# Feed-forwards with one 512-column matmul over both parts of the input, in a fused kernel of three transformer blocks

## The reference

```python
def _swiglu(x, w_gate, w_up, w_down):
    return (jax.nn.silu(x @ w_gate) * (x @ w_up)) @ w_down

x = x + 0.5 * _swiglu(_rmsnorm(x, ffn1_norm[l]), ffn1_w_gate[l], ffn1_w_up[l], ffn1_w_down[l])
```

## Time and profile before

| | us |
|---|---|
| median of 3 runs (lowest to highest) | 4005.26 (3999.87 to 4008.55) |
| span of the profiled execution | 4004.4 |
| PE busy | 3909.7 (98%) |
| PE loading weights | 3793.3 (95%) |
| DVE busy | 2736.3 (68%) |
| ACT busy | 1987.8 (50%) |

### The profile page before, as it was taken

The page is one execution under the profiler, slowest core; times in us unless marked ns, Lnnn a source line. Parts: engine busy times, 40 slices in busy tenths (PEclk is TensorE's granted clock), DMA queues, the critical chain, the costliest instruction groups (busy, mean ns, idle before and its releaser), DMA issues.

```text
span 4004.4 us, 78708 instructions
## 1 busy us (share of the span) xinstructions
PE 3909.7 (98%) x34150; PEld 3793.3 (95%) x34150; DVE 2736.3 (68%) x4071; ACT 1987.8 (50%) x2620; POOL 212.2 (5%) x277
## 2 busy tenths in 40 slices
PE   8999999999999999999999999999999999999999
PEld 8979999889998999999997999999998899999999
DVE  6566665666655656567555799956756699974855
ACT  5445444454544545465435545754444544764443
POOL 0011000110002000010023000000000000000000
PEclk9999999999999999999998999999999999999999
DMA  6534555345555455534550455456654455455754
GB/s 237 192 115 151 192 190 190 133 148 195 181 194 182 160 199 184 195 133 173 191 204 34 159 194 181 177 199 233 229 196 153 158 177 193 175 182 202 265 199 158
DMA packets 114791, 720.78 MB, mean 180 GB/s; under 512 B 13328, under 2 KB 13664, under 8 KB 32784
## 3 DMA queue, kind: packets, MB, share of 16 engines
q1 hardware_dynamic: 90144, 652.25, 45.9%
q10 hardware_dynamic: 19200, 37.01, 2.5%
q0 software_dynamic: 5104, 26.49, 1.9%
HBM read 692.48 MB, written 23.22 MB: 179 GB/s over the span
## 4 chain that ended last, share of the span: by engine, by line
PE 87%; DVE 7%; ACT 4%; issue 1%; POOL 0%; DMA 0%; ACTq 0%; DVEq 0%; POOLq 0%
PE psum L655 26%; PE psum L657 26%; PE psum L656 26%; PE psum L1408 3%; DVE slab_low L1916 2%; ACT slab_high L1427 2%; DVE h_parts L2219 1%; PE psum L1065 1%; PE psum L1048 1%; PE psum L875 1%; PE psum L1078 1%; ACT room L1670 1%; DVE room L2248 0%; DVE room L2253 0%; PE psum L1349 0%
## 5 line engine op out<-in xcount | busy, mean ns | idle before, releaser
L1916 DVE TENSOR_TENSOR slab_low<-slab,slab_high 128x2048 fp32r<-128x2048 f32 x622 | 1423.2, 2289 | 738.8 <-ACT slab_high L1427 736.6
L655 PE MATMUL psum<-h_parts,slab_high 128*128 128x256 f32 x5632 | 1578.2, 280 | 28.9 <-DVE h_parts L2219 18.6
L1427 ACT ACTIVATE slab_high<-slab 128x2048 fp32r<-128x2048 f32 x622 | 1189.3, 1912 | 785.4 <-PE psum L657 721.1
L656 PE MATMUL psum<-h_parts,slab_high 128*128 128x256 f32 x5632 | 1556.5, 276 | 0.0
L657 PE MATMUL psum<-h_parts,slab_low 128*128 128x256 f32 x5632 | 1556.1, 276 | 0.0
L655 PEld LDWEIGHTS psum<-h_parts,slab_high 128*128 128x128 f32 x5632 | 1063.5, 189 | 48.8 <-issue 24.0
L655 PE MATMUL psum<-hidden_parts,slab_high 128*128 128x256 f32 x3840 | 1063.5, 277 | 11.4 <-DVE hidden_parts L2166 4.8
L656 PEld LDWEIGHTS psum<-h_parts,slab_high 128*128 128x128 f32 x5632 | 1063.5, 189 | 2.4 <-issue 2.2
L657 PEld LDWEIGHTS psum<-h_parts,slab_low 128*128 128x128 f32 x5632 | 1062.8, 189 | 0.0
L656 PE MATMUL psum<-hidden_parts,slab_high 128*128 128x256 f32 x3840 | 1058.0, 276 | 0.0
L657 PE MATMUL psum<-hidden_parts,slab_low 128*128 128x256 f32 x3840 | 1058.0, 276 | 0.0
(11 more groups left out here) (346 smaller groups left out, 3326.0 us busy)
## 6 DMA issues: line engine op xcount, KB each, us to landing
slab<-in_up SPq DMA_DIRECT2D x176, 1024.0 KB, 4.8
slab<-in_keys_up SPq DMA_DIRECT2D x128, 1024.0 KB, 4.8
slab<-in_keys_down SPq DMA_DIRECT2D x128, 1024.0 KB, 4.8
slab<-in_down SPq DMA_DIRECT2D x88, 1024.0 KB, 4.8
slab<-in_w_in SPq DMA_DIRECT2D x16, 1024.0 KB, 4.8
slab<-in_wq SPq DMA_DIRECT2D x16, 1024.0 KB, 4.8
peer_gates<-room ACTq DMA_DIRECT2D x64, 256.0 KB, 2.3
room<-peer_gates ACTq DMA_DIRECT2D x64, 256.0 KB, 5.4
```

What stands on the lines that cost most here:

```text
L655: nc.tensor.matmul(out, lhs[0], rhs[0], start=first, stop=False, **options)
L656: nc.tensor.matmul(out, lhs[0], rhs[1], start=False, stop=False, **options)
L1427: nc.scalar.activation(k.high[m % PARTS][:, 0:width], k.slabs[m % RING][:, 0:width], ACT.Copy).then_inc(k.rounded.up())
L1916: nc.vector.tensor_tensor(k.low[m % RING][:, 0:width], k.slabs[m % RING][:, 0:width], k.high[m % PARTS][:, 0:width], ALU.subtract).then_in ...
```

## The change

A new helper, `halves`, makes a product of two matmuls. The high weight tile meets both parts of the input in one matmul of 512 moving columns, which leaves high x high in the first 256 columns of a bank and high x low in the second 256; the low tile then meets the high part alone, 256 columns, added to the first half. It is used in all 22 up slabs and in the first 9 of the 11 down slabs. Since a bank now holds two halves of each result, they are added elsewhere:

- ups: ACT copies the second halves of a pair out of PSUM (`second_copied`), DVE adds the first halves to that copy (`halves_added`) and then scales the sum in SBUF;
- downs: after nine slabs the second halves are complete. During slab 9 (counted from 0) DVE adds half of them to x, one instruction for each pair of banks, and PE waits for each of them ahead of row 19 of that slab (`second_added`). Slabs 9 and 10 keep the three-matmul product.

ACT's tick moves: the copy of pair t-2 comes first, then the rounding of slab t+2, the hidden row t-3, the silu of t-2. Roundings and rests that stood after the ticks now stand in two more ticks.

```diff
+    def halves(self, out, lhs, both, first, last):
+        nc = self.k.nc
+        nc.tensor.matmul(out.rearrange("p (a t) -> p a t", a=2), lhs[0], both, start=first, stop=False)
+        return nc.tensor.matmul(out[:, 0:T], lhs[1], both[:, 0, :], start=False, stop=last)
...
 TensorE.ffn, ups
-                        mm = self.product(pair[:, a], [part[:, a, c, :] for part in w], (k.h[:, c, 0, :], k.h[:, c, 1, :]), c == 0, c == DC - 1)
+                        mm = self.halves(pair[:, a], [part[:, a, c, :] for part in w], k.h[:, c], c == 0, c == DC - 1)
...
 TensorE.ffn, downs
-                    mm = self.product(k.banks[c][:, 0:T], (high[:, cols], low[:, cols]), (k.hidden[:, f, 0, :], k.hidden[:, f, 1, :]),
-                                      f == 0, False)
+                    if r < FC // 2 - 2:
+                        mm = self.halves(k.banks[c], (high[:, cols], low[:, cols]), k.hidden[:, f], f == 0, f == FC - 5)
+                        continue
+                    if e == 1 and n % 2 == 0:
+                        nc.tensor.wait_ge(k.second_added.sem, k.second_added.at(n // 2 + 1))
+                    mm = self.product(k.banks[c][:, 0:T], (high[:, cols], low[:, cols]), (k.hidden[:, f, 0, :], k.hidden[:, f, 1, :]), False, False,
+                                      skip_group_check=True)
+                    if e == 0 and n % 2:
+                        mm.then_inc(k.second_left.up())
...
 ScalarE.ffn
-        for tick in range(FC + 2):
-            if (2 if fold else 0) <= tick < FC:
+        for tick in range(FC + 3):
+            if 2 <= tick < FC + 2:
+                f = tick - 2
+                nc.scalar.wait_ge(k.slab_done.sem, k.slab_done.at(f + 1))
+                if f >= 2:
+                    nc.scalar.wait_ge(k.multiplied.sem, k.multiplied.at(f - 1))
+                nc.scalar.activation(v.both[:, f % 2], k.bank_pairs[(f + k.first_pair) % 4][:, :, T:2 * T], ACT.Copy).then_inc(k.second_copied.up())
+            if (2 if fold else 0) <= tick < FC + 2:
                 self.round_slab()
...
 VectorE.ffn
-                nc.vector.wait_ge(k.slab_done.sem, k.slab_done.at(f + 1))
-                if f >= 2:
-                    nc.vector.wait_ge(k.multiplied.sem, k.multiplied.at(f - 1))
-                nc.vector.tensor_tensor(both, k.bank_pairs[(f + k.first_pair) % 4][:, :, 0:T], v.rstd.unsqueeze(1).to_broadcast([P, 2, T]),
-                                        ALU.mult).then_inc(k.up_scaled.up())
-        for r in range(FC // 2 - 1):
+                nc.vector.wait_ge(k.second_copied.sem, k.second_copied.at(f + 1))
+                nc.vector.tensor_tensor(both, k.bank_pairs[(f + k.first_pair) % 4][:, :, 0:T], both, ALU.add).then_inc(k.halves_added.up())
+                nc.vector.wait_ge(k.halves_added.sem, k.halves_added.at(f + 1))
+                nc.vector.tensor_tensor(both, both, v.rstd.unsqueeze(1).to_broadcast([P, 2, T]), ALU.mult).then_inc(k.up_scaled.up())
+        for r in range(FC // 2 - 3):
             self.rest_slab()
+        for j in range(DC // 2):
+            both = k.x[:, 2 * j:2 * j + 2, :]
+            nc.vector.wait_ge(k.second_left.sem, k.second_left.at(j + 1))
+            nc.vector.scalar_tensor_tensor(out=both, in0=k.bank_pairs[j][:, :, T:2 * T], scalar=0.5, in1=both,
+                                           op0=ALU.mult, op1=ALU.add).then_inc(k.second_added.up())
```

More of the change, by code:

```diff
@@ L232, in __init__ @@
         self.pair_done = signal("pair_done")
+        self.second_copied, self.halves_added = signal("second_copied"), signal("halves_added")
+        self.second_left, self.second_added = signal("second_left"), signal("second_added")
         self.hidden_rounded, self.hidden_ready = signal("hidden_rounded"), signal("hidden_ready")
@@ L691, in ffn @@
             at = (f + k.first_pair) % 4
-            pair = k.bank_pairs[at][:, :, 0:T]
+            pair = k.bank_pairs[at]
             if f >= 4:
@@ L703, in ffn @@
                 firsts, lag = [], FIRST_LAG if first else DC if k.before == "ffn" else 2
-                pairs = [k.bank_pairs[g + k.first_pair][:, :, 0:T] for g in range(2)]
+                pairs = [k.bank_pairs[g + k.first_pair] for g in range(2)]
                 for step in range(DC + lag):
@@ L714, in ffn @@
                         for a in range(2):
-                            mm = self.product(pairs[g][:, a], [part[:, a, c, :] for part in firsts[g]], (k.h[:, c, 0, :], k.h[:, c, 1, :]), c == 0, c == DC - 1)
+                            mm = self.halves(pairs[g][:, a], [part[:, a, c, :] for part in firsts[g]], k.h[:, c], c == 0, c == DC - 1)
                         if c == DC - 1:
@@ L742, in ffn @@
                     mm = self.product(k.banks[2 * j + c][:, 0:T], (high[:, cols], low[:, cols]),
-                                      (k.hidden[:, 2 * r + e, 0, :], k.hidden[:, 2 * r + e, 1, :]), False, e == 1)
+                                      (k.hidden[:, 2 * r + e, 0, :], k.hidden[:, 2 * r + e, 1, :]), False, e == 1, skip_group_check=True)
                     if e == 1 and c == 1 and j < 3:
@@ L1500, in ffn @@
                 nc.scalar.dma_start(k.bias_views.table[0:32, :], k.dram["bias_table"]).then_inc(k.small.up(), 16)
-            if tick >= 2:
-                f = tick - 2
+            if tick >= 3:
+                f = tick - 3
                 nc.scalar.wait_ge(k.multiplied.sem, k.multiplied.at(f + 1))
                 nc.scalar.activation(k.hidden[:, f, 0, :], v.acts[:, f % 2, :], ACT.Copy).then_inc(k.hidden_rounded.up())
-            if 1 <= tick <= FC:
-                f = tick - 1
+            if 2 <= tick < FC + 2:
+                f = tick - 2
                 gate = v.both[:, f % 2, 0]
@@ L1509, in ffn @@
                 nc.scalar.activation(gate, gate, ACT.Silu).then_inc(k.gated.up())
-        for r in range(FC // 2):
+        for r in range(FC // 2 - 2):
             self.round_slab()
@@ L1978, in ffn @@
         for tick in range(FC + 2):
-            if tick < FC and not (fold and tick == 1):
+            if not (fold and tick == 1):
                 self.rest_slab()
@@ L2011, in ffn @@
                 both = v.both[:, f % 2]
-                nc.vector.wait_ge(k.slab_done.sem, k.slab_done.at(f + 1))
-                if f >= 2:
-                    nc.vector.wait_ge(k.multiplied.sem, k.multiplied.at(f - 1))
-                nc.vector.tensor_tensor(both, k.bank_pairs[(f + k.first_pair) % 4][:, :, 0:T], v.rstd.unsqueeze(1).to_broadcast([P, 2, T]),
-                                        ALU.mult).then_inc(k.up_scaled.up())
-        for r in range(FC // 2 - 1):
-            self.rest_slab()
+                nc.vector.wait_ge(k.second_copied.sem, k.second_copied.at(f + 1))
[3 more added lines that the diff above has]
+        for r in range(FC // 2 - 3):
+            self.rest_slab()
+        for j in range(DC // 2):
[3 more added lines that the diff above has]
+                                           op0=ALU.mult, op1=ALU.add).then_inc(k.second_added.up())
+        second_added = k.second_added.at(DC // 2)
         self.owed = True
@@ L2027, in finish @@
                 nc.vector.wait_ge(k.slab_done.sem, all_done)
+            if j == 0:
+                nc.vector.wait_ge(k.second_added.sem, second_added)
             nc.vector.scalar_tensor_tensor(out=both, in0=k.bank_pairs[j][:, :, 0:T], scalar=0.5, in1=both,
```

## The result

The changed kernel takes 4126.15 us (median of 4 runs, 4123.59 to 4132.25), the kernel before 4006.08 beside it: a ratio of 1.030 (95% interval 1.0287 to 1.0317). The forecast of 4016 us had the direction and a tenth of the size (0.3% for 3.0%), and its range (to 4040) does not hold the time.

A forecast was written before the change was run, and what follows sets the result against it. PE was taken to bound the kernel: 4004.4 - 45.8 gained in products + 57.9 of new waits = 4016.5, predicted as 4016 us, 0.3% slower; range 3999 to 4040.

The forecast's parts named there:

- The product: PE's 512-column plus 256-column matmul in changed slabs: 0.217 + 0.111 = 0.328 us against 0.340, gaining 0.012 each.
- its ends: Bounds for one high-and-low-tile pair of matmuls on PE: 0.325 us gains 0.015, 0.340 us gains nothing.
- The slowed wide matmul: 512-column matmul slowed by load beside it, towards 2 x 0.113; pair 0.331 to 0.340, 4028 to 4062 us; chance 0.09.
- Ups to downs: Down slab 0, seventh product: PE waits for pair 21's scaling, 2.9 us in each of eight feed-forwards.
- Last slab but one: PE ahead of row 19 waits for DVE's additions behind the rest of slab 33: 2.5 us, eight times.
- Starts: Start of each feed-forward: PE waits longer for the next rest, 6 x 1.5 + 3.4 + 2.3 = 14.7 us more.
- The clock: Sixteen new PE waits of 2.5 to 2.9 us lower the clock: 14 us more, 4030 us; chance 0.05.
- Mid-stage cover: Middle of a run of ups: nothing waits, 3.7 us to spare; DVE would be next with 1 us to spare.
- the rival below my forecast: PE's columns and loads overlap slightly better, 0.325 to 0.3265 us per product: 4005 to 4011 us; chance 0.27.
- the chain from a slab's end to the next rest: Among the ups: ACT's rounding through copy, DVE's sum and scaling, then rest: 6.8 us, within two slabs of PE, 10.5 us.

The follow-up runs named there:

- the mended run with narrow matmuls: Changed kernel with ACT's copy of pair 21 and DVE's second-half additions moved earlier, each 512-column matmul split in two of 256: 4031.2 us.
- the mended runs: Changed kernel with ACT's copy of pair 21 and DVE's second-half additions moved earlier: 4080.0 us with 512-column matmuls, 4031.2 with three of 256.

## Why the prediction was wrong

- **The product (0.328 us forecast, 0.353 measured) is the step that failed**, and its ends, 0.325 to 0.340, do not hold it: the wide matmul takes 0.235 where I had 0.217, the narrow one behind it 0.118 where I had 0.111. The same matmuls done narrow give 48.8 us back (4078.7 to 4029.9); forecast was a gain of 45.8. That is 94.6 of the 110 us between forecast and time. I took 0.217 from the earlier trace rows for 512 columns, but that format makes two passes over 256 columns in it, and says nothing of 512 different ones. (By their starts these matmuls are 0.2157 apart; the 3.47 us hold the end of the last one too.) And I read the earlier trace rows as if loads set the pace; with loads of a quarter the product stayed at 0.348.
- **The slowed wide matmul**, which I gave 0.09 and ended at 2 x 0.113 = 0.226, is what happened, beyond that end. Its reason (the load that reads beside it) holds for at most 0.006 of the 0.013.
- **Ups to downs**: 2.9 forecast; 8.39 - 5.65 = 2.74 without a fall of the clock. Right, and so is the order of the chain in the rows above.
- **Last slab but one**: 2.5 forecast; 8.08 - 5.44 = 2.64. Right.
- **Starts**: 14.7 forecast; 10.4 by the lines on slab_low, and the mended run with narrow matmuls leaves about 13 (25.5 us over the kernel before, of it 8 x 1.6 at the ups-to-downs slab). Nearly right.
- **The clock**, a rival with 0.05, came on top of the forecast and not in its place: nine more falls of 1.5 us, 14 us. Seven stand behind the 2.5 us wait for the scaling, two behind the additions, and the mended runs have none there. The row that spoke against it, 2.42 us at the full clock, was a single case: in the changed kernel the same wait, 2.49 us ahead of 284.17, has the lower clock from 283.83 on. Trainium skill, "TensorE: Matmul & The Clock Gate", section "HAM oscillation — how this bites in real kernels", describes longer waits between bursts; here waits of 2.5 us had the same effect in seven places of eight.
- **Mid-stage cover**: right. DVE has 1.25 us left per slab and PE waits for nobody.
- **Trainium skill, "TensorE: Matmul & The Clock Gate", section "Back-to-back issue gap"**: its N/2.4 + 2.5, which the section gives for a matmul by itself, makes 0.216 for 512 columns. The two-pass matmuls of the earlier trace rows keep to that (0.2157); a wide matmul of this format takes 0.224 or more in every run. Its N/1.2 for the lower clock agrees with the 0.213 above. The rule was one ground for the rival below my forecast, which fell with it.
- **Two small sums** are off and change nothing: the chain from a slab's end to the next rest adds up to 6.6 us, not 6.8, and 4016.5 with the 0.9 of the median is 4017.

The sum by measured terms: 4004.4 + 48.8 (width) + 48.0 (the mended waits with their clock) + 25.5 (starts, and what is left of ups to downs) = 4126.7. The last three are differences of spans, so they add up by themselves; the 25.5 is taken apart only by the waits above.

No version tried beats the kernel before: with the best wide matmul seen (0.224) and the best narrow one (0.113), never seen together, a product would save 0.003, 12 us, against the 25 us that the mended order still costs.

## What to carry to other kernels

Before merging matmuls to save their number, ask whether the surplus over columns belongs to the instruction or to the column. A stretch at the lower clock shows that there is a surplus at the full one, not whose it is; a run in which only the shape changes tells it (here 0.231 for 512 columns against 0.227 for two of 256). A stream that has found its pace is measured anew when its shape changes, and a bound taken from a slower format is not a bound. Where one engine's new step feeds another's, put it ahead of the long step that waits for later data; a wait of 2.5 us in dense work costs 1.5 more where the clock falls behind it.

## What was not expected of the hardware

- A matmul of 512 columns of this format takes 0.224 to 0.241 us at the full clock and 0.427 at the lower one, which is columns alone.
- The place in SBUF where the moving rows start is worth 3% of this kernel's time: 4140.9 us at 0, 4012.2 at 240, with only that number changed (what lies behind the rows in SBUF moves along).
- The pace goes in turns of fixed length (225, 231, 237 ns; at 112 a steady 235 and 118), and at 248 it differs between the feed-forwards of one run, so a mean over a slab in each is needed to compare two places.
